# Even stage: five low parts of weight slots made by GpSimd instead of VectorE

## The chip, the cores and the metric

The kernel runs on one core of one Trainium2 chip. The time is that of one execution on the device in microseconds; runs of a kernel are compared by their median. Engines are named as in the profile: PE (TensorE; PEld is its weight load), DVE (VectorE), ACT (ScalarE), POOL (GpSimd), SP (SyncE, which issues the transfers).

## What is computed

Four transformer layers on one sequence of 256 tokens of width 1024, all in float32: two layers of a first block (SwiGLU, a mixer of three branches, SwiGLU), then an "even" layer and an "odd" layer of a second block. The change touches the even layer:

```python
h = rms_norm(x, even_norm_g[i])
proj = h @ even_w_in[i]
q, k, v, z_a, u, z_b = jnp.split(proj, ...)
q = rms_norm(q.reshape(bsz, L, SB_HEADS, SB_HEAD_DIM), sb_q_norm_g[i])
k = rms_norm(k.reshape(bsz, L, SB_HEADS, SB_HEAD_DIM), sb_k_norm_g[i])
o_a = stick_breaking_attention(q, k, v).reshape(bsz, L, SB_WIDTH) * jax.nn.silu(z_a)
o_b = s5_mixer(u, ...) * jax.nn.silu(z_b)      # a diagonal complex state space model, a scan over time
x = x + jnp.concatenate([o_a, o_b], axis=-1) @ even_w_out[i]
```

## The kernel before

**Weights.** All weight matrices are cut into slots of 128 x 2048 float32 (1 MB). A product in full precision is made of three products of a shorter format: each weight w is split into a high part (w copied to fp32r) and a low part (w minus its high part), and `exact3` issues high*high, high*low and low*high (L257 to L259). A slot so goes through four hands: SP loads it into `w_raw` (`load`), ACT copies it to `w_high` (`split_high`, L224), DVE subtracts into `w_low` (`split_low`, L231), and PE multiplies, 48 matmuls for most slots. Three buffers of each kind are used in turn (`RING = 3`): slot n may be loaded when the low part of slot n-3 is made, and its high part may be made when PE is through with slot n-3. Every step waits on a semaphore count; `made(n)` says how many low (or high) parts are made once slot n is.

**Order.** Each engine runs its own list of instructions in the order in which the Python code writes it, and nothing is reordered. The even layer has 29 slots: 0 and 1 give u, 2 and 3 z_b, 4 to 7 z_a, 8 to 11 q, 12 to 15 k, 16 to 19 v, 20 the GLU, 21 to 28 the output. Class `Even` has one method for each engine; each is a loop over n with slot n's own work and, by `after(n)`, the high part (ACT) or low part (DVE) of slot n+3, since slots are three ahead. On DVE an n consists of: the evacuation of slot n's bank (`evac`, L2193 or L2196; for q and k `normalised`, L2203 and L2204), `after(n)`, and at n = 2, 3, 5, 6, 8, 9, 11, 13 one of the eight batches of the state space scan (`scan(0)` to `scan(7)`; at 8, 11 and 13 ahead of `after`). A scan is two products that read PSUM (L2216, L2217; the second releases the PSUM banks, `x_taken`), then ten instructions whose inputs are all in SBUF (L2219, L2220, four scans L2226, L2228 to L2231).

**Who waits for that.** PE, after slot 9, makes the next input of the scans (L2378) into banks that the L2217 of `scan(4)` must have read. In the middle of slots 10 to 17 it transposes a normalised row block (L2358), which needs L2204 and, three times, `skip` (L2236). Before each slot it waits for the low part. ACT makes, in order for each n, the squares and the root for `normalised` (L2078, L2084), the high part of slot n+3, and the silu of z (L2099), which waits for DVE's `evac`.

**GpSimd** works only in the setup and in the two mixers of the first block (bias tables at L1077, windowed sums at L1092). It has nothing to do in the even layer.

Of the kernel before, what the change touches and what calls it, by code (L numbers as in the profile page):

```python
# [19 lines left out]
DEPTH = 2  # L20
# [4 lines left out]
RING = 3  # L25
# [96 lines left out]
class Core:  # L122

    def __init__(self, nc, ctx, weights):
        self.nc = nc
        self.sems = []
        self.ctx = ctx
        self.weights = weights
        sb = lambda name, shape, dt=F32: ctx.enter_context(nc.sbuf_tensor(name, shape, dt))
        self.raw = sb("w_raw", [P, RING, SLOT])  # L130
        self.vec = sb("vectors", [P, V_WIDTH])
        self.tab = sb("table", [P, T_WIDTH])
        self.constants = sb("constants", [P, 2])
# [72 lines left out]
    def made(self, n):  # L206
        return sum(SLOT_PARTS[:n + 1]) + max(n + 1 - len(SLOT_PARTS), 0)

    def load(self, sp, n):
        j = n % RING  # L210
        if n >= RING:
            sp.wait_ge(self.lo_made, self.made(n - RING))
        sp.dma_start(self.raw[:, j, 0:SIZES[n]], self.weights[n][:, 0:SIZES[n]]).then_inc(self.landed[j], 16)
# [12 lines left out]
    def split_low(self, dve, n):  # L226
        if n >= N_SLOTS:
            return
        dve.wait_ge(self.hi_made, self.made(n))
        if n not in self.narrow:  # L230
            dve.tensor_tensor(self.slot(self.wl, n), self.slot(self.raw, n),  # L231
                              self.slot(self.wh, n).bitcast(F32), ALU.subtract).then_inc(self.lo_made, 1)
            return
        gained, gain, f = self.narrow[n]
        if f:
            dve.tensor_tensor(self.slot(self.wl, n)[:, 0:f], self.slot(self.raw, n)[:, 0:f],
                              self.slot(self.wh, n)[:, 0:f].bitcast(F32), ALU.subtract)
        dve.tensor_tensor(gained, self.slot(self.raw, n)[:, f:].rearrange("p (k n) -> p k n", k=DT),
                          gain.unsqueeze(2).to_broadcast([P, DT, QUAD]), ALU.mult).then_inc(self.lo_made, 1)

    def whole(self, n):
# [41 lines left out]
def project(c, pe, bank, n, kt, norm=None, tokens=False, width=FC, x=None, midway=None):  # L283
# [3 lines left out]
    if n >= len(SLOT_PARTS):  # L287
        pe.wait_ge(c.lo_made, c.made(n))
    for k in range(kt):
# [19 lines left out]
def values_half(c, pe, banks, n, half, between=None):  # L309


    wh, wl = c.weights_at(n, DT // 2, 2 * FC)
    pe.wait_ge(c.lo_made, c.made(n))
    for i, bank in enumerate(banks):
# [196 lines left out]
class Ffn:  # L511
# [108 lines left out]
    def tensor(self, pe):  # L620
        c, b, base = self.c, self.b, self.base
# [11 lines left out]
        def down(s):  # L633
            n = base + down_at(s)
            wh, wl = c.weights_at(n, 2, D)
            hh, hl = b.hh[:, s % 2], b.hl[:, s % 2]
            pe.wait_ge(c.lo_made, c.made(n))
            pe.wait_ge(*self.hid_low(s + 1))
# [31 lines left out]
class FfnApart(Ffn):  # L670
# [78 lines left out]
    def tensor(self, pe):  # L749
# [12 lines left out]
        for m in range(FF_STEPS):  # L762
            n = base + 2 * FF_STEPS + m
            wh, wl = c.weights_at(n, SLOT_TILES, FC)
            pe.wait_ge(c.lo_made, c.made(n))
            for p in range(4):
# [279 lines left out]
class Mixer:  # L1046
# [406 lines left out]
    def tensor(self, pe):  # L1453
# [95 lines left out]
        def out_part(n, kks):  # L1549
            u = unit_of(n)  # L1550
            b = bank_free(u) if kks[0] == 0 else unit_bank(u)
            wh, wl = c.weights_at(base + n, DT, FC)
            pe.wait_ge(c.lo_made, c.made(base + n))
            for kk in kks:
# [12 lines left out]
        wh, wl = c.weights_at(n, DT, KV_RANK)  # L1567
        pe.wait_ge(c.lo_made, c.made(n))
        for kk in range(DT):
# [28 lines left out]
        n = base + S_UQ  # L1598
        pe.wait_ge(c.lo_made, c.made(n))
        pe.wait_ge(*t["latent_lo"](2))  # L1600
# [9 lines left out]
        n = base + S_UKV  # L1610
        pe.wait_ge(c.lo_made, c.made(n))
        wh, wl = (c.slot(w, n) for w in (c.wh, c.wl))
# [34 lines left out]
        for n in range(S_BRANCH, S_OUT):  # L1647
# [3 lines left out]
            at = (0, 4, 0)[b]  # L1651
            pe.wait_ge(c.lo_made, c.made(base + n))
            pe.wait_ge(*(t["o_read"](HEADS // 2), t["d_l"](1), t["pool_l"](1))[b])
# [345 lines left out]
class Even:  # L1999
# [326 lines left out]
    def tensor(self, pe):  # L2326
# [8 lines left out]
        def glu(part):  # L2335
            n = base + A_GLU
            wh, wl = c.weights_at(n, UT, S5_W)
            pe.wait_ge(c.lo_made, c.made(n))
            pe.wait_ge(self.y_low, 1)
# [125 lines left out]
        for n in range(A_OUT, EVEN_SLOTS):  # L2465
            b = bank_free(even_unit(n))
            wh, wl = c.weights_at(base + n, EVEN_K, P)
            pe.wait_ge(c.lo_made, c.made(base + n))
            for kk in range(EVEN_K):
# [44 lines left out]
class Odd:  # L2514
# [275 lines left out]
    def tensor(self, pe):  # L2790
# [49 lines left out]
        def heads(n, which):  # L2840
# [3 lines left out]
            wh, wl = c.weights_at(base + n, DT, FC)  # L2844
            pe.wait_ge(c.lo_made, c.made(base + n))
            for h in which:
# [8 lines left out]
        for n in range(G_OUT):  # L2855
# [8 lines left out]
            elif n == G_R:  # L2864
                pe.wait_ge(c.lo_made, c.made(base + n))
                four_columns(pe, c.bank(b, SEQ), c.narrow[base + n][0], c.h).then_inc(c.done, 1)
                self.norm.mean(pe)
            elif n == 0:
                wh, wl = c.weights_at(base, DT, FC)
                pe.wait_ge(c.lo_made, c.made(base))  # L2870
                for kk in range(DT):
# [42 lines left out]
        for n in range(G_OUT, ODD_SLOTS):  # L2914
            if n == G_OUT + 1:
                continue
            if n == ODD_SLOTS - 1:
                b = bank_free(n)
                wh, wl = c.weights_at(base + n, DT, FC)
                pe.wait_ge(c.lo_made, c.made(base + n))  # L2920
                for i in range(2):
# [32 lines left out]
def model_kernel(nc, x, first, pos, table, weights, vectors, second, out):  # L2954
    with ExitStack() as ctx:
# [32 lines left out]
        with nc.Block() as block:  # L2988
# [229 lines left out]
```

## Time and profile before

| what | value |
|---|---|
| median of 3 runs | 1457.62 us (1457.6 to 1457.7) |
| the profiled execution: own time / span | 1457.46 us / 1455.5 us |
| granted TensorE clock | 1.00 throughout |
| PE busy | 1447.2 us, 99% |
| DVE busy | 1057.0 us, 73% |
| ACT busy | 783.2 us, 54% |
| POOL busy | 34.9 us, 2% |
| chain that ended last | PE 93%, DVE 6%, issue 1% |

Busy time is an average over stages; the even layer runs from about 1157 to 1357 us of the span. The profiler's span begins and ends inside the measured time, so an execution's own time is about 2 us more than its span. The span of an instruction includes time in which it is held after it was started. Starts of neighbouring instructions on one engine can overlap the end of the one ahead by some hundredths of a microsecond.

### The profile page before, as it was taken

To read this page: it belongs to the slowest core of one execution; us is meant where nothing else is said; L and a number is where in the kernel's file an instruction comes from. 1 tells how busy PE (TensorE), PEld (TensorE's weight loads), DVE (VectorE), ACT (ScalarE), POOL (GpSimd) and SP (SyncE) were. 2 spreads that over 40 slices of the span, in tenths; PEclk is the share of its full clock that TensorE was granted. 3 is DMA by queue.
4 is the path that set the end of the run, shared out by engine and by line. 5 is a ranking of instruction groups with operands and counts; after the bars stand their busy time and mean duration, and the time that the engine had idled before them with its cause. 6 is when DMAs were issued, how large, how long until landed. Compare 5 with 4: busy or idle time off the path is not lost.

```text
span 1455.5 us, 28504 instructions
## 1 busy us (share of the span) xinstructions
PE 1447.2 (99%) x12414; PEld 1403.4 (96%) x12414; DVE 1057.0 (73%) x1462; ACT 783.2 (54%) x1012; POOL 34.9 (2%) x41
## 2 busy tenths in 40 slices
PE   9999999999999999999999999999999999999999
PEld 9999998999999999999999899999999999989978
DVE  7766676897876655766548689888787799766844
ACT  6444555565554443544446566555645645775753
POOL 0000000210000000000000020000000000000000
PEclk9999999999999999999999999999999999999999
DMA  8655545444555555555554544466555454425541
GB/s 331 225 186 191 191 149 207 145 146 154 194 196 193 201 183 197 200 188 190 201 186 140 194 147 149 170 220 219 203 191 187 149 188 157 145 97 177 198 141 59
DMA packets 38843, 261.36 MB, mean 180 GB/s; under 512 B 4672, under 2 KB 5184, under 8 KB 9152
## 3 DMA queue, kind: packets, MB, share of 16 engines
q1 hardware_dynamic: 38576, 259.54, 52.4%
q8 instruction: 98, 1.61, 0.4%
q14 instruction: 25, 0.20, 0.0%
q10 hardware_dynamic: 144, 0.00, 0.0%
HBM read 258.48 MB, written 1.05 MB: 178 GB/s over the span
## 4 chain that ended last, share of the span: by engine, by line
PE 93%; DVE 6%; issue 1%; ACT 0%; POOL 0%; POOLq 0%
PE ps L257 29%; PE ps L258 28%; PE ps L259 28%; DVE w_low L231 2%; PE ps L1518 1%; DVE scratch L2226 1%; PE ps L1509 0%; PE ps L1491 0%; DVE even_s_rot L2228 0%; PE ps L1533 0%; DVE even_s_rot L2229 0%; DVE even_s_rot L2216 0%; DVE even_s_rot L2217 0%; PE ps L923 0%; PE ps L2812 0%
## 5 line engine op out<-in xcount | busy, mean ns | idle before, releaser
L224 ACT ACTIVATE w_high<-w_raw 128x2048 fp32r<-128x2048 f32 (+1 forms) x243 | 457.3, 1883 | 472.1 <-PE ps L259 469.0
L231 DVE TENSOR_TENSOR w_low<-w_raw,w_high 128x2048 fp32r<-128x2048 f32 (+1 forms) x240 | 545.3, 2273 | 203.2 <-ACT w_high L224 202.8
L257 PE MATMUL ps<-x,w_high 128*128 128x256 f32 x2224 | 622.4, 280 | 0.5 <-DVE w_low L231 0.4
L259 PE MATMUL ps<-x,w_low 128*128 128x256 f32 x2224 | 616.9, 277 | 0.0
L258 PE MATMUL ps<-x,w_high 128*128 128x256 f32 x2224 | 616.7, 277 | 0.0
L257 PEld LDWEIGHTS ps<-x,w_high 128*128 128x128 f32 x2224 | 418.3, 188 | 5.0 <-issue 3.3
L259 PEld LDWEIGHTS ps<-x,w_low 128*128 128x128 f32 x2224 | 418.8, 188 | 0.0
L258 PEld LDWEIGHTS ps<-x,w_high 128*128 128x128 f32 x2224 | 418.5, 188 | 0.3
L257 PE MATMUL ps<-ffn_hid,w_high 128*128 128x256 f32 x528 | 145.7, 276 | 0.0
L258 PE MATMUL ps<-ffn_hid,w_high 128*128 128x256 f32 x528 | 145.7, 276 | 0.0
L259 PE MATMUL ps<-ffn_hid,w_low 128*128 128x256 f32 x528 | 145.7, 276 | 0.0
L257 PEld LDWEIGHTS ps<-ffn_hid,w_high 128*128 128x128 f32 x528 | 99.1, 188 | 0.0
L258 PEld LDWEIGHTS ps<-ffn_hid,w_high 128*128 128x128 f32 x528 | 99.1, 188 | 0.0
L259 PEld LDWEIGHTS ps<-ffn_hid,w_low 128*128 128x128 f32 x528 | 99.1, 188 | 0.0
L257 PE MATMUL ps<-w_high,x 128*128 128x512 f32 (+1 forms) x256 | 87.8, 343 | 0.8 <-DVE w_low L231 0.8
L259 PE MATMUL ps<-w_high,x 128*128 128x512 f32 (+1 forms) x256 | 85.4, 334 | 0.0
L258 PE MATMUL ps<-w_low,x 128*128 128x512 f32 (+1 forms) x256 | 85.4, 334 | 0.0
L257 PE MATMUL ps<-mix_y_high,w_high 128*128 128x256 f32 x224 | 62.6, 279 | 0.8 <-issue 0.8
L259 PE MATMUL ps<-mix_y_high,w_low 128*128 128x256 f32 x224 | 62.3, 278 | 0.0
L258 PE MATMUL ps<-mix_y_low,w_high 128*128 128x256 f32 x224 | 62.3, 278 | 0.0
L257 PEld LDWEIGHTS ps<-w_high,x 128*128 128x128 f32 x256 | 48.1, 188 | 7.9 <-issue 2.4
L259 PEld LDWEIGHTS ps<-w_high,x 128*128 128x128 f32 x256 | 48.0, 188 | 5.2
(478 smaller groups left out, 2086.7 us busy)
## 6 DMA issues: line engine op xcount, KB each, us to landing
w_raw<-in_weights SPq DMA_DIRECT2D x229, 1024.0 KB, 4.9
w_raw<-in_weights SPq DMA_DIRECT2D x10, 768.0 KB, 4.2
setup_first<-in_first SPq DMA_DIRECT2D x8, 256.0 KB, 4.9
w_raw<-in_weights SPq DMA_DIRECT2D x4, 512.0 KB, 5.0
even_second_vectors<-in_second SPq DMA_DIRECT2D x1, 1836.0 KB, 7.4
w_raw<-in_weights SPq DMA_DIRECT2D x2, 640.0 KB, 3.9
resid<-in_x SPq DMA_DIRECT2D x1, 1024.0 KB, 10.7
out<-resid SPq DMA_DIRECT2D x3, 256.0 KB, 3.0
```

The lines of the kernel that those rows point to most:

```text
L224: act.activation(self.slot(self.wh, n)[:, f], self.slot(self.raw, n)[:, f], ACT.Copy).then_inc(self.hi_made, 1)
L231: dve.tensor_tensor(self.slot(self.wl, n), self.slot(self.raw, n), self.slot(self.wh, n).bitcast(F32), ALU.subtract).then_inc(self.lo_made, 1)
L257: pe.matmul(out, ah, bh, start=start, stop=False, skip_group_check=True)
L258: pe.matmul(out, ah, bl, start=False, stop=False, skip_group_check=True)
L259: return pe.matmul(out, al, bh, start=False, stop=stop, skip_group_check=True)
L1518: mm = pe.transpose(c.bank(B_T)[:, i * P:(i + 1) * P], m.pr[:, 0, i * P:(i + 1) * P], ident)
L2226: ins = dve.tensor_tensor_scan(s[:, i, part, :], r, pc[:, i, part, :], 0.0, ALU.mult, ALU.add)
```

## The change

The low parts of the even layer's slots 6, 8, 10, 12 and 14 are made by GpSimd, with the same subtraction of 128 x 2048, in five instructions at the end of its list. They count on a semaphore of their own, `lo_made_pool`. A function `low(n)` gives the semaphore and the count that tell that slot n's low part is made; all waits on it (TensorE, and SyncE ahead of the load of slot n+3) use that. Nothing else is moved.

```diff
@@ constants
+POOL_LOWS = [DEPTH * LAYER_SLOTS + n for n in (6, 8, 10, 12, 14)]
@@ Core
+    def low(self, n):
+
+        if n in POOL_LOWS:
+            return self.lo_pool, POOL_LOWS.index(n) + 1
+        return self.lo_made, self.made(n) - sum(x < n for x in POOL_LOWS)
+
     def load(self, sp, n):
         j = n % RING
         if n >= RING:
-            sp.wait_ge(self.lo_made, self.made(n - RING))
+            sp.wait_ge(*self.low(n - RING))
...
     def split_low(self, dve, n):
-        if n >= N_SLOTS:
+        if n >= N_SLOTS or n in POOL_LOWS:
             return
...
+    def split_low_on_pool(self, pool, n):
+
+        pool.wait_ge(self.hi_made, self.made(n))
+        pool.tensor_tensor(self.slot(self.wl, n), self.slot(self.raw, n),
+                           self.slot(self.wh, n).bitcast(F32), ALU.subtract).then_inc(self.lo_pool, 1)
...
@@ project, values_half and every other place where TensorE waits for a slot
-        pe.wait_ge(c.lo_made, c.made(n))
+        pe.wait_ge(*c.low(n))
@@ block.gpsimd
                 for l in range(DEPTH):
                     stages[3 * l + 1].gpsimd(pool)
+                for n in POOL_LOWS:
+                    c.split_low_on_pool(pool, n)
```

On VectorE, from the end of `scan(3)` to `scan(4)`, before (L2196 is the evacuation of slot 7, L231 the low part of slot 10, L2236 `skip(0)`):

```order
L2230 TENSOR_TENSOR scratch<-even_s_rot 128x2x128
L2231 TENSOR_TENSOR scratch<-even_s_rot 128x2x128
L2196 TENSOR_TENSOR even_za<-ps,rstd 128x512
L231 TENSOR_TENSOR w_low<-w_raw,w_high 128x2048
L2236 SCALAR_TENSOR_TENSOR even_u<-even_u,even_second_vectors,ps 128x256
L2203 RECIPROCAL even_q_sums<-even_q_sums 128x4
L2204 TENSOR_TENSOR even_second_vectors<-ps,even_q_sums 128x512
L2216 TENSOR_TENSOR even_s_rot<-ps,even_cos 128x512
```

and now (line numbers are 8 to 14 higher in the changed file; L2210 is L2196, L2250 is L2236, L2230 is L2216):

```order
L2244 TENSOR_TENSOR scratch<-even_s_rot 128x2x128
L2245 TENSOR_TENSOR scratch<-even_s_rot 128x2x128
L2210 TENSOR_TENSOR even_za<-ps,rstd 128x512
L2250 SCALAR_TENSOR_TENSOR even_u<-even_u,even_second_vectors,ps 128x256
L2217 RECIPROCAL even_q_sums<-even_q_sums 128x4
L2218 TENSOR_TENSOR even_second_vectors<-ps,even_q_sums 128x512
L2230 TENSOR_TENSOR even_s_rot<-ps,even_cos 128x512
```

The low part of slot 10 is gone from between the evacuation and `skip(0)`.

On VectorE, from the end of `scan(4)` to `scan(5)`, before (the first L231 is the low part of slot 11, the second that of slot 12):

```order
L2231 TENSOR_TENSOR scratch<-even_s_rot 128x2x128
L231 TENSOR_TENSOR w_low<-w_raw,w_high 128x2048
L2203 RECIPROCAL even_q_sums<-even_q_sums 128x4
L2204 TENSOR_TENSOR even_second_vectors<-ps,even_q_sums 128x512
L231 TENSOR_TENSOR w_low<-w_raw,w_high 128x2048
L2216 TENSOR_TENSOR even_s_rot<-ps,even_cos 128x512
```

and now:

```order
L2245 TENSOR_TENSOR scratch<-even_s_rot 128x2x128
L239 TENSOR_TENSOR w_low<-w_raw,w_high 128x2048
L2217 RECIPROCAL even_q_sums<-even_q_sums 128x4
L2218 TENSOR_TENSOR even_second_vectors<-ps,even_q_sums 128x512
L2230 TENSOR_TENSOR even_s_rot<-ps,even_cos 128x512
L2231 TENSOR_TENSOR even_s_rot<-ps,even_sin 128x512
```

The low part of slot 11 stays where it was, that of slot 12 is gone.

The end of GpSimd's list before:

```order
L1092 TENSOR_TENSOR mix_arena<-mix_pool_in 128x4x256
L1092 TENSOR_TENSOR mix_arena<-mix_arena 128x3x256
L1092 TENSOR_TENSOR mix_arena<-mix_arena 128x2x256
L1092 TENSOR_TENSOR mix_arena<-mix_arena 128x256
L1077 TENSOR_SCALAR mix_bias<-distance 128x384 x6
```

and now:

```order
L1106 TENSOR_TENSOR mix_arena<-mix_arena 128x3x256
L1106 TENSOR_TENSOR mix_arena<-mix_arena 128x2x256
L1106 TENSOR_TENSOR mix_arena<-mix_arena 128x256
L1091 TENSOR_SCALAR mix_bias<-distance 128x384 x6
L252 TENSOR_TENSOR w_low<-w_raw,w_high 128x2048 x5
```

Five subtractions of 128 x 2048 follow the last bias tables.

## Rows read from the trace of the kernel before

**Rows 1.** Even stage, busy us of PE, PEld, DVE, ACT, POOL; PEclk, DMA share, GB/s.

```profile
1200.00:1250.00 50.00, 48.33 (x521) 46.46 (x520) 46.46 (x81) 27.91 (x75) 0.00 (x0) 1.00 0.41 143
```

**Rows 2.** TensorE timeline: start, us, instruction, [idle before <-releaser].

```profile
1220.74 0.49 PE L2378 MATMUL ps<-even_u,even_b_ahead 32*128 32x128 f32 x4 [0.25 <-DVE even_s_rot L2217]
...
1227.84 0.28 PE L257 MATMUL ps<-w_high,x 128*128 128x256 f32 x1
...
1237.26 0.66 PE L2358 MATMUL ps<-table,even_second_vectors 128*128 128x128 f32 x4 [0.64 <-DVE even_second_vectors L2204]
...
1249.88 0.36 PE L257 MATMUL ps<-w_high,x 128*128 128x256 f32 x1 [0.77 <-DVE w_low L231]
...
1253.29 0.63 PE L2358 MATMUL ps<-table,even_second_vectors 128*128 128x128 f32 x4 [0.34 <-DVE even_u L2236]
```

**Rows 3.** w_low, VectorE, 1155 to 1262 us: ns min/median/max.

```profile
L231 DVE TENSOR_TENSOR w_low<-w_raw,w_high x16: 2271/2282/2293, 1160.3 to 1259.5; 128x2048 fp32r<-128x2048 f32 x16
```

**Rows 4.** DMA issues of the page: KB each, us from issue to landing.

```profile
w_raw<-in_weights SPq DMA_DIRECT2D x229, 1024.0 KB, 4.9
```

**Rows 5.** GpSimd groups by form: busy us, mean ns of one, idle before.

```profile
L1092 POOL TENSOR_TENSOR mix_arena<-mix_pool_in 128x1024 f32<-128x1024 f32 x2 | 3.8, 1894 | 82.0 <-DVE mix_pool_in L1262 82.0
...
L1092 POOL TENSOR_TENSOR mix_arena<-mix_arena 128x512 f32<-128x512 f32 x2 | 2.3, 1168 | 0.2
```

**Rows 6.** Timelines of GpSimd, then of VectorE, in the first mixer.

```profile
261.50 1.89 POOL L1092 TENSOR_TENSOR mix_arena<-mix_pool_in 128x1024 f32<-128x1024 f32 x1 [40.98 <-DVE mix_pool_in L1262]
263.48 3.47 POOL L1092 TENSOR_TENSOR mix_arena<-mix_arena 128x768 f32<-128x768 f32 x1
310.68 1.17 POOL L1077 TENSOR_SCALAR mix_bias<-distance 128x384 f32<-128x384 f32 x1 [5.75 <-DVE mix_max L1284]
...
261.47 0.42 DVE L1284 CUSTOM_DVE_ANT_0 mix_scores<-ps,table 128x256 f32<-128x256 f32 x1
...
261.93 1.49 DVE L1288 TENSOR_SCALAR mix_neg_max<-mix_max 128x2 f32<-128x2 f32 x1
263.34 2.28 DVE L231 TENSOR_TENSOR w_low<-w_raw,w_high 128x2048 fp32r<-128x2048 f32 x1
...
310.71 2.62 DVE L231 TENSOR_TENSOR w_low<-w_raw,w_high 128x2048 fp32r<-128x2048 f32 x1
```

**Rows 7.** ScalarE timeline, even stage: the high parts of slots 6, 8, 10, 12.

```profile
1182.63 1.93 ACT L224 ACTIVATE w_high<-w_raw 128x2048 fp32r<-128x2048 f32 x1 [2.90 <-PE ps L259]
...
1195.94 1.91 ACT L224 ACTIVATE w_high<-w_raw 128x2048 fp32r<-128x2048 f32 x1
...
1207.19 1.91 ACT L224 ACTIVATE w_high<-w_raw 128x2048 fp32r<-128x2048 f32 x1
...
1221.80 1.90 ACT L224 ACTIVATE w_high<-w_raw 128x2048 fp32r<-128x2048 f32 x1
```

**Rows 8.** VectorE timeline, even stage: the scans and their neighbours.

```profile
1184.10 0.69 DVE L2228 TENSOR_TENSOR even_s_rot<-scratch,even_cos 128x512 f32<-128x512 f32 x1
1184.71 0.69 DVE L2229 TENSOR_TENSOR even_s_rot<-scratch,even_sin 128x512 f32<-128x512 f32 x1
...
1186.23 0.69 DVE L2193 TENSOR_TENSOR even_second_vectors<-ps,rstd 128x512 f32<-128x512 f32 x1
...
1190.35 0.43 DVE L2219 TENSOR_TENSOR even_s_rot<-even_s_rot 128x256 f32<-128x256 f32 x1
...
1201.60 0.43 DVE L2219 TENSOR_TENSOR even_s_rot<-even_s_rot 128x256 f32<-128x256 f32 x1
...
1210.05 0.43 DVE L2219 TENSOR_TENSOR even_s_rot<-even_s_rot 128x256 f32<-128x256 f32 x1
...
1220.01 0.68 DVE L2217 TENSOR_TENSOR even_s_rot<-ps,even_sin 128x512 f32<-128x512 f32 x1
...
1225.05 2.29 DVE L231 TENSOR_TENSOR w_low<-w_raw,w_high 128x2048 fp32r<-128x2048 f32 x1
...
1241.79 0.69 DVE L2216 TENSOR_TENSOR even_s_rot<-ps,even_cos 128x512 f32<-128x512 f32 x1 [1.57 <-PE ps L2378]
```

More of the change, by code:

```diff
@@ L147, in __init__ @@
         self.landed = [self.sem(f"landed{j}") for j in range(RING)]
+        self.lo_pool = self.sem("lo_made_pool")
         self.hi_made, self.lo_made, self.done = self.sem("hi_made"), self.sem("lo_made"), self.sem("bank_filled")
@@ L312, in values_half @@
     wh, wl = c.weights_at(n, DT // 2, 2 * FC)
-    pe.wait_ge(c.lo_made, c.made(n))
+    pe.wait_ge(*c.low(n))
     for i, bank in enumerate(banks):
@@ L636, in down @@
             hh, hl = b.hh[:, s % 2], b.hl[:, s % 2]
-            pe.wait_ge(c.lo_made, c.made(n))
+            pe.wait_ge(*c.low(n))
             pe.wait_ge(*self.hid_low(s + 1))
@@ L764, in tensor @@
             wh, wl = c.weights_at(n, SLOT_TILES, FC)
-            pe.wait_ge(c.lo_made, c.made(n))
+            pe.wait_ge(*c.low(n))
             for p in range(4):
@@ L1552, in out_part @@
             wh, wl = c.weights_at(base + n, DT, FC)
-            pe.wait_ge(c.lo_made, c.made(base + n))
+            pe.wait_ge(*c.low(base + n))
             for kk in kks:
@@ L1567, in tensor @@
         wh, wl = c.weights_at(n, DT, KV_RANK)
-        pe.wait_ge(c.lo_made, c.made(n))
+        pe.wait_ge(*c.low(n))
         for kk in range(DT):
@@ L1598, in tensor @@
         n = base + S_UQ
-        pe.wait_ge(c.lo_made, c.made(n))
+        pe.wait_ge(*c.low(n))
         pe.wait_ge(*t["latent_lo"](2))
@@ L1610, in tensor @@
         n = base + S_UKV
-        pe.wait_ge(c.lo_made, c.made(n))
+        pe.wait_ge(*c.low(n))
         wh, wl = (c.slot(w, n) for w in (c.wh, c.wl))
@@ L1651, in tensor @@
             at = (0, 4, 0)[b]
-            pe.wait_ge(c.lo_made, c.made(base + n))
+            pe.wait_ge(*c.low(base + n))
             pe.wait_ge(*(t["o_read"](HEADS // 2), t["d_l"](1), t["pool_l"](1))[b])
@@ L2337, in glu @@
             wh, wl = c.weights_at(n, UT, S5_W)
-            pe.wait_ge(c.lo_made, c.made(n))
+            pe.wait_ge(*c.low(n))
             pe.wait_ge(self.y_low, 1)
@@ L2467, in tensor @@
             wh, wl = c.weights_at(base + n, EVEN_K, P)
-            pe.wait_ge(c.lo_made, c.made(base + n))
+            pe.wait_ge(*c.low(base + n))
             for kk in range(EVEN_K):
@@ L2844, in heads @@
             wh, wl = c.weights_at(base + n, DT, FC)
-            pe.wait_ge(c.lo_made, c.made(base + n))
+            pe.wait_ge(*c.low(base + n))
             for h in which:
@@ L2864, in tensor @@
             elif n == G_R:
-                pe.wait_ge(c.lo_made, c.made(base + n))
+                pe.wait_ge(*c.low(base + n))
                 four_columns(pe, c.bank(b, SEQ), c.narrow[base + n][0], c.h).then_inc(c.done, 1)
@@ L2869, in tensor @@
                 wh, wl = c.weights_at(base, DT, FC)
-                pe.wait_ge(c.lo_made, c.made(base))
+                pe.wait_ge(*c.low(base))
                 for kk in range(DT):
@@ L2919, in tensor @@
                 wh, wl = c.weights_at(base + n, DT, FC)
-                pe.wait_ge(c.lo_made, c.made(base + n))
+                pe.wait_ge(*c.low(base + n))
                 for i in range(2):
```

## The prediction

> **What bounds the kernel now.** I read three things in this order. The busy times of one stretch come first: from 1200 to 1250 us, in the even stage, PE is busy 48.33 us and DVE 46.46 [rows 1]. PE ends the program, so I look for its idle time next: among the moved instructions it waits four times with any weight, 0.25 us for a scan's product, 0.64 us for a normalised row, 0.77 us for the low part of slot 14 and 0.34 us for L2236 [rows 2]. That is 2.0 us. Two things are to be seen here: every releaser is VectorE, and the whole prize is small. VectorE is barely fast enough, and if it is a microsecond later, TensorE stops at these same places for a microsecond more. Third I read what GpSimd and VectorE do to each other in the first mixer, the place where both work [rows 6].
>
> **What moves.** Five subtractions of 128x2048 leave VectorE, where one takes 2.28 us [rows 3]. Its neighbour starts 0.08 us before it ends, as L2229 at 1184.71 does against 1184.10 + 0.69 [rows 8], so each frees 2.2 us of VectorE, 11 us in all. GpSimd, with 0.00 us of work in that stretch [rows 1], gets them. TensorE and SyncE wait as often as before, only on another semaphore: 0 us. The loads of slots 9, 11, 13, 15 and 17 now follow GpSimd's subtraction. By the times below the latest against need is the load of slot 15, issued at about 1231; it takes 4.9 us [rows 4], and slot 15's high part can't be made before TensorE is through with slot 12, after 1237.26 [rows 2]. That cover hides it; without it a late load would hold the high part by as much.
>
> **What one costs on GpSimd.** No row has 2048 elements. 1024 took 1.89 us, 512 took 1.17 [rows 5]. Going on by that step, 0.725 us for 512 elements, gives 1.89 + 1.45 = 3.35 us, the lower end; doubling 1.89 gives 3.79, the upper. VectorE can be held for all of that or a little less. I call the hold H and take **H = 3.4 us**, nearest to the step, with 3.2 and 3.8 as ends.
> The Trainium skill (GPSIMD Engine Reference, "Elementwise — side-by-side cycle accounting") gives 4497 ns for a tensor_tensor of 2048 fp32 elements; this trace's 1024 in 1.89 us speaks for less. By that price the sum below would end near 1466 us.
>
> **Is there room for it?** The high part of slot 12 is made at 1221.80 + 1.90 = 1223.7 us [rows 7]. TensorE starts slot 11 at 1227.84 and is in the middle of slot 12 at 1237.26, after 0.64 us of waiting [rows 2]: 8.8 us for a slot and a half, so slot 12 starts at about 1233.7. That leaves 10 us for an instruction of 3.4 to 3.8. The others have much the same, since slots are made three ahead. So TensorE won't wait for GpSimd; what counts is what GpSimd does to VectorE.
>
> **What they do to each other** [rows 6]. While GpSimd's 1024-element addition ran (261.50 to 263.39), a VectorE instruction on PSUM and one SBUF operand took 0.42 us, but a TENSOR_SCALAR of 2 elements took 1.49 and ended when the addition ended. Then w_low started ahead of GpSimd's 768-element addition: w_low took its usual 2.28 us, the addition 3.47, more than the 1.89 of the larger one. So they take turns, by whole instructions. Where a short GpSimd instruction started just ahead of w_low (310.68 against 310.71), w_low took 2.62: a subtraction with two SBUF inputs is held as well.
> The Trainium skill (SBUF — State Buffer, "Who interferes with whom") has this rule: a VectorE instruction with two SBUF inputs contends with a GpSimd instruction that reads SBUF, the one that comes first keeps the lock to its end, and the other blocks. By that rule, the trace agrees, and it speaks against the change.
>
> **The sum.** In each scan L2216 and L2217 read PSUM, the ten instructions L2219 to L2231 have SBUF inputs alone. I let GpSimd take its turn at the first boundary between two VectorE instructions after its high part is made. Shifts are against before; times of high parts are in rows 7, of VectorE in rows 8.
> - Slot 6: high part ends at 1184.56, within scan 0. VectorE is held 3.4 and saves 2.2: +1.2 us.
> - Slot 8: the high part ended at 1197.85, behind a silu that waits for VectorE's L2196; now 1199.05, so the hold lasts until 1202.45. L2219 of scan 2 stood at 1201.60: +0.9 us.
> - Slot 10: high part, likewise behind a silu, 1209.1 + 0.9 = 1210.0, hold until 1213.4. L2219 of scan 3 stood at 1210.05: +3.4 us. The dropped w_low gives nothing back here, since what follows waits for a chain that starts with the shifted evacuation of slot 7: silu, squares and root on ScalarE, L2204, then L2217 of scan 4, which moves from 1220.01 by 3.4. TensorE waited for that one before [rows 2] and now waits **3.4 us more**.
> - Slot 12: the high part is made at 1227.1, within scan 4, and VectorE is held 3.4 once more. w_low of slot 11 ends at 1227.34 + 3.4 + 3.4 = 1234.1; TensorE wants it at 1227.84 + 3.4 = 1231.2: **2.9 us more**.
> - Slot 14: its turn comes while VectorE waits for TensorE, ahead of 1241.79; it holds nothing. The two w_low dropped at slots 12 and 14 put VectorE ahead, and TensorE gets back 0.64 + 0.77 + 0.34 = **1.75 us**.
> As a formula, (3H - 6.8) + (H - 0.5) - 1.75 = 4H - 9.05 = **+4.55 us**; +3.75 with H = 3.2, +6.15 with 3.8. The profiled execution took 1457.46 us (its span 1455.5, 2.0 lie around it), 0.16 below the median of 1457.62. 1457.46 + 4.55 = **1462.0 us**. A measurement can tell about 0.2% from no change, here 2.9 us.
>
> **Rivals.**
> 1. VectorE keeps its turn while instructions with two SBUF inputs follow each other. For it: each starts before the one ahead ends [rows 8]. Against it: rows 6 show whole instructions taking turns; neither shows GpSimd asking amid such a run. Slot 6 is then made from 1186.23, at L2193, to 1189.6. L2219 of scan 1, due at 1190.35 - 2.2, waits for that: -0.75 us. Slot 8 in the same way holds until 1200.5 against 1201.60: -1.1. Slot 10: high part at 1208.0, hold until 1211.5 against 1210.05: +1.45, all on TensorE as above. Slot 12 waits until scan 4 and w_low of slot 11 are through and holds nobody who matters. 1.45 - 1.75 = -0.3: **1457.2 us**, not slower. What decides is who gets the first boundary inside a scan.
> 2. They don't hold each other in these forms, and VectorE is 2.2 us earlier five times. The four waits go: 1457.46 - 2.0 = **1455.5 us**, still within 0.2%. Rows 6 speak against it. For 2.9 us the stage would have to give more than TensorE idles in it.
> 3. Turns as in the forecast but a longer instruction, since no GpSimd row writes fp32r. A fifth above the upper end is H = 4.4: +8.55, **1466.0 us**.
> 4. The change doesn't do what it says: the orders exclude it.
>
> **Chances.** Forecast 0.50, of which 0.03 come out below 2.9 us; rival 1 0.34, of which 0.03 come out slower with a long H; rival 2 0.07, of which 0.04 go beyond the edge; rival 3 0.09. Slower 0.47 + 0.03 + 0.09 = 0.59, faster 0.04, same 0.37. The range leaves out rival 2 and half of rival 3, about 0.12 in all, and takes in rival 1 with H = 3.2, some 0.7 below its 1457.2: 1456.4 to 1466.0. The forecast's own range is 1461.2 to 1463.6.
>
> **What would show it.** Five GpSimd rows of 128x2048, 3.4 to 3.8 us besides waits. In VectorE's timeline L2228 or L2229 of scan 0 and one such instruction of scan 4 grown to about 4 us, L2219 of scans 2 and 3 grown too. TensorE waiting some 3.6 us at L2378 near 1221 us and 3 us for slot 11's low part, and not at slot 14. If GpSimd's rows stretch to 4 to 8 us instead and no VectorE row inside a scan has grown, rival 1 holds; if neither has, rival 2. If a GpSimd row passes 9 us, TensorE waits for GpSimd itself, and the reasoning is wrong at "is there room".

## The result, and the profile after

The changed kernel takes 1465.87 us (median of 4 runs, 1465.66 to 1466.57) against 1457.66 us for the kernel before (4 runs, 1457.6 to 1458.11): ratio 1.0059, 95% interval 1.0047 to 1.0072, **8.2 us slower**. The forecast was 1462.0, its own range 1461.2 to 1463.6. The direction, the places and the mechanism came as predicted; one term, the length of GpSimd's subtraction, was too small. The profiled execution took 1466.57 us, its span is 1464.4, 8.9 more than before.

The page of the changed kernel, busy times and the chain that ended last (lines of kernel.py are 8 to 14 higher than before: L252 is GpSimd's new subtraction, L239 is w_low, L271 to L273 the products of `exact3`, L2230, L2231, L2233, L2242 to L2245 were L2216, L2217, L2219, L2228 to L2231; L2392 was L2378, L2372 was L2358, and L2407, the products of a finished scan, was L2393):

```profile
PE 1449.9 (99%) x12414; PEld 1405.9 (96%) x12414; DVE 1061.1 (72%) x1457; ACT 782.9 (53%) x1012; POOL 58.6 (4%) x46
...
PE 93%; DVE 5%; issue 1%; ACT 1%; DMA 1%; SPq 0%
```

GpSimd has 23.7 us more, and VectorE, from which 5 x 2.2 = 11 us were taken, is busier than before (1057.0); the chain is TensorE's as before. VectorE's figure can grow although work left it, because an instruction that is held counts as busy while it is held; the rows below show four of these. The stretch of [rows 1] in the changed kernel, same columns:

```profile
1200.00:1250.00 50.00, 42.22 (x397) 40.59 (x396) 45.18 (x64) 22.42 (x54) 15.83 (x4) 0.93 0.39 129
```

VectorE is nearly as busy as in [rows 1] with 64 instructions in place of 81, TensorE got 397 matmuls done in place of 521, and its granted clock fell below 1.00, which nothing in the trace of before had shown. GpSimd's timeline, 1100 to 1300 us (start, us, instruction, idle before and its releaser):

```profile
1184.61 4.78 POOL L252 TENSOR_TENSOR w_low<-w_raw,w_high 128x2048 fp32r<-128x2048 f32 x1 [292.12 <-ACT w_high L232]
1200.26 4.70 POOL L252 TENSOR_TENSOR w_low<-w_raw,w_high 128x2048 fp32r<-128x2048 f32 x1 [10.87 <-ACT w_high L232]
1212.39 4.61 POOL L252 TENSOR_TENSOR w_low<-w_raw,w_high 128x2048 fp32r<-128x2048 f32 x1 [7.43 <-ACT w_high L232]
1230.57 4.96 POOL L252 TENSOR_TENSOR w_low<-w_raw,w_high 128x2048 fp32r<-128x2048 f32 x1 [13.57 <-ACT w_high L232]
1248.44 4.65 POOL L252 TENSOR_TENSOR w_low<-w_raw,w_high 128x2048 fp32r<-128x2048 f32 x1 [12.91 <-ACT w_high L232]
```

They take 4.6 to 5.0 us, not 3.4 to 3.8. VectorE's timeline beside them:

```profile
1184.86 5.08 DVE L2243 TENSOR_TENSOR even_s_rot<-scratch,even_sin 128x512 f32<-128x512 f32 x1
...
1201.73 3.52 DVE L2233 TENSOR_TENSOR even_s_rot<-even_s_rot 128x256 f32<-128x256 f32 x1
...
1212.55 0.68 DVE L2231 TENSOR_TENSOR even_s_rot<-ps,even_sin 128x512 f32<-128x512 f32 x1
1213.26 4.01 DVE L2233 TENSOR_TENSOR even_s_rot<-even_s_rot 128x256 f32<-128x256 f32 x1
...
1231.04 4.77 DVE L2244 TENSOR_TENSOR scratch<-even_s_rot 128x256 f32<-128x256 f32 x1
...
1236.18 2.29 DVE L239 TENSOR_TENSOR w_low<-w_raw,w_high 128x2048 fp32r<-128x2048 f32 x1
```

Four rows have grown: L2243 of scan 0 from 0.69 to 5.08 us, a hold of 4.39; L2233 of scans 2 and 3 from 0.43 to 3.52 and 4.01; L2244 of scan 4 from 0.42 to 4.77, 4.35. Each ends within 0.6 us of a GpSimd row's end. L2231 of scan 3, which reads PSUM, ran through beside GpSimd in its usual 0.68. The four holds make 15.4 us, less the 11 taken away 4.4, and VectorE's busy time grew by 4.1. Slot 14's subtraction held none. And TensorE, each row of the stage with idle time ahead of it, after the start of the scans:

```profile
1213.29 0.49 PE L2392 MATMUL ps<-even_u,even_b_ahead 32*128 32x128 f32 x4 [0.66 <-DVE even_s_rot L2231]
...
1221.19 0.49 PE L2407 MATMUL ps<-even_u,even_b_c 128*128 128x128 f32 x2 [0.90 <-DVE scratch L2245]
...
1227.54 0.80 PE L2392 MATMUL ps<-even_u,even_b_ahead 32*128 32x128 f32 x4 [4.85 <-DVE even_s_rot L2231]
...
1238.62 0.36 PE L271 MATMUL ps<-w_high,x 128*128 128x256 f32 x1 [1.37 <-DVE w_low L239]
```

Against [rows 2]: the product that began at 1220.74 begins at 1227.54, 6.8 later; slot 11's first product, 1227.84, now begins at 1238.62, 10.8 later. The 0.64, 0.77 and 0.34 us at and after slot 12 have no rows any more. 10.8 - 1.75 = 9.0, and the span grew by 8.9.

### The profile page after: what moved, and what is told of

Same layout as the page of the kernel before. It is cut to its first block, busy times and chain, and to the rows that moved or that the text cites. A ratio compares the mean times of both kernels' runs of the same rounds, so it can differ in the third digit from the quotient of the medians.

```text
span 1464.4 us, 28504 instructions
## 1 busy us (share of the span) xinstructions
PE 1449.9 (99%) x12414; PEld 1405.9 (96%) x12414; DVE 1061.1 (72%) x1457; ACT 782.9 (53%) x1012; POOL 58.6 (4%) x46
## 4 chain that ended last, share of the span: by engine, by line
PE 93%; DVE 5%; issue 1%; ACT 1%; DMA 1%; SPq 0%
PE ps L271 29%; PE ps L272 28%; PE ps L273 28%; DVE w_low L239 1%; PE ps L1532 1%; DVE even_s_rot L2233 1%; DVE even_s_rot L2243 1%; DMA w_raw<-in_weights 1%; PE ps L1523 0%; DVE scratch L2240 0%; PE ps L1505 0%; PE ps L1547 0%; PE ps L2826 0%; PE ps L2841 0%; PE ps L2838 0%
## 5 line engine op out<-in xcount | busy, mean ns | idle before, releaser
L239 DVE TENSOR_TENSOR w_low<-w_raw,w_high 128x2048 fp32r<-128x2048 f32 (+1 forms) x235 | 533.8, 2272 | 204.2 <-ACT w_high L232 203.9
L271 PE MATMUL ps<-x,w_high 128*128 128x256 f32 x2224 | 622.4, 280 | 0.9 <-DVE w_low L239 0.4
L273 PE MATMUL ps<-x,w_low 128*128 128x256 f32 x2224 | 616.7, 277 | 0.0
L271 PEld LDWEIGHTS ps<-x,w_high 128*128 128x128 f32 x2224 | 418.4, 188 | 5.4 <-issue 3.3
L273 PEld LDWEIGHTS ps<-x,w_low 128*128 128x128 f32 x2224 | 418.6, 188 | 0.0
L271 PE MATMUL ps<-ffn_hid,w_high 128*128 128x256 f32 x528 | 145.7, 276 | 0.0
L273 PE MATMUL ps<-ffn_hid,w_low 128*128 128x256 f32 x528 | 145.7, 276 | 0.0
L271 PEld LDWEIGHTS ps<-ffn_hid,w_high 128*128 128x128 f32 x528 | 99.1, 188 | 0.0
L273 PEld LDWEIGHTS ps<-ffn_hid,w_low 128*128 128x128 f32 x528 | 99.1, 188 | 0.0
L271 PE MATMUL ps<-w_high,x 128*128 128x512 f32 (+1 forms) x256 | 88.7, 347 | 1.4 <-DVE w_low L239 1.4
L273 PE MATMUL ps<-w_high,x 128*128 128x512 f32 (+1 forms) x256 | 86.1, 337 | 0.0
L271 PE MATMUL ps<-mix_y_high,w_high 128*128 128x256 f32 x224 | 62.6, 279 | 0.8 <-issue 0.8
L273 PE MATMUL ps<-mix_y_high,w_low 128*128 128x256 f32 x224 | 62.2, 278 | 0.0
L271 PEld LDWEIGHTS ps<-w_high,x 128*128 128x128 f32 x256 | 48.9, 191 | 8.7 <-issue 3.6
L273 PEld LDWEIGHTS ps<-w_high,x 128*128 128x128 f32 x256 | 48.8, 191 | 5.2
```

The source lines that it names most:

```text
L271: pe.matmul(out, ah, bh, start=start, stop=False, skip_group_check=True)
L273: return pe.matmul(out, al, bh, start=False, stop=stop, skip_group_check=True)
```

## The experiments

Each is the changed kernel with one edit, except where it says before; "..." stands for lines left out. Times are medians, beside runs of the kernel before on the same chip, whose own medians lay between 1457.32 and 1457.91.

**1. The relief alone.** What do five subtractions fewer on VectorE bring, if nobody makes them?

```diff
-            return self.lo_pool, POOL_LOWS.index(n) + 1
+            return self.hi_made, self.made(n)
...
-                for n in POOL_LOWS:
-                    c.split_low_on_pool(pool, n)
```

`weights_at` gives the high part in place of the missing low one for these five slots, so the results of these five slots lack their low parts.

> The five low parts are left out altogether (TensorE takes the high part a second time in their place and waits for the high part only), so VectorE is relieved as in the change and GpSimd does nothing. Theory (the loss is all due to GpSimd holding VectorE): the four waits of TensorE, 2.0 us, go, and the time is 1455.6 us, 2.0 under before; no VectorE row in the scans is longer than before. Rival (the relief is worth more, or moving work off VectorE costs something by itself, for instance through the loads that start earlier): 1453 or less, or 1457.5 or more.

Measured: 1455.12 us against 1457.91, ratio 0.9982 (0.9973 to 0.9990), 2.8 us faster. The 1200 to 1250 us row:

```profile
1200.00:1250.00 50.00, 50.00 (x538) 48.43 (x538) 39.12 (x72) 29.03 (x75) 0.00 (x0) 1.00 0.41 146
```

TensorE doesn't idle here at all. The prize was small, as the prediction had it (2.0 us of waits); the spans differ by 2.3. The rest, 8.2 + 2.8 = 11 us, is what GpSimd's work costs.

**2. Slot 14 alone, and 3. slot 12 alone.**

```diff
-POOL_LOWS = [DEPTH * LAYER_SLOTS + n for n in (6, 8, 10, 12, 14)]
+POOL_LOWS = [DEPTH * LAYER_SLOTS + n for n in (14,)]
```

and the same with `(12,)`.

> Only slot 14's low part goes to GpSimd. Theory (whole turns, first come first served, a turn of 4.45 us): the high part is made at 1237.4, while w_low of slot 13 (1237.13 to 1239.4) has its turn, so GpSimd runs from 1239.4 to 1243.9, mostly while VectorE waits for TensorE; L2219 of scan 6 is held 0.7 us, w_low of slot 14 is saved, 2.2: the waits at slot 14 and before L2358 (0.77 + 0.34) go, 1456.5 us, 1.1 under before. Rival (GpSimd gets in ahead of w_low of slot 13, or holds more than whole turns): w_low of slot 13 ends 4.4 later, TensorE waits 2 to 3 us for it, 1459 to 1460.

> Only slot 12's low part goes to GpSimd. Theory (turn of 4.45 us at the first boundary within scan 4): w_low of slot 11 ends at 1227.34 + 4.45 = 1231.8 against 1227.84, TensorE waits 4.0 us there and gets 0.64 back before L2358: +3.3, 1460.9 us; if TensorE's clock falls after that wait, up to 2.5 us more. Rival (one turn alone is harmless, the loss of the change needs the three turns before it): within 1 us of before.

Measured for slot 14: 1456.32 us, ratio 0.9988 (0.9979 to 0.9997), 1.6 us **faster** than before. GpSimd, then VectorE:

```profile
1236.36 6.33 POOL L252 TENSOR_TENSOR w_low<-w_raw,w_high 128x2048 fp32r<-128x2048 f32 x1 [344.64 <-ACT w_high L232]
...
1235.89 2.28 DVE L239 TENSOR_TENSOR w_low<-w_raw,w_high 128x2048 fp32r<-128x2048 f32 x1
1241.88 1.10 DVE L2233 TENSOR_TENSOR even_s_rot<-even_s_rot 128x256 f32<-128x256 f32 x1
```

GpSimd waits for the w_low that had started first (to 1238.17), then works 4.5 us, mostly while VectorE waits for TensorE and reads PSUM; only 0.7 us of VectorE is held. TensorE's waits of 0.77 and 0.34 us [rows 2] have no rows any more: 1.1 of the 1.6. Slot 12 alone: 1462.46 us, ratio 1.0035 (1.0022 to 1.0049), 4.5 slower. VectorE's L2244 grows to 4.76 us, slot 11's w_low is late, and TensorE waits; the windows behind it show the clock (columns as in [rows 1]):

```profile
1224.20 4.76 DVE L2244 TENSOR_TENSOR scratch<-even_s_rot 128x256 f32<-128x256 f32 x1
...
1231.77 0.36 PE L271 MATMUL ps<-w_high,x 128*128 128x256 f32 x1 [3.71 <-DVE w_low L239]
...
1232.00:1234.00 2.00, 2.00 (x13) 2.00 (x13) 1.97 (x4) 0.00 (x0) 0.00 (x0) 0.61 0.59 135
1234.00:1236.00 2.00, 2.00 (x12) 2.00 (x12) 1.93 (x7) 0.00 (x0) 0.00 (x0) 0.54 1.04 438
```

3.71 less the 0.64 that is no longer waited for is 3.1 us. In the next 4 us TensorE runs at half clock, 1.2 GHz, most of the time: 2 x 0.39 + 2 x 0.46 = 1.7 us lost. Together 4.8, measured 4.5. So the same instruction is worth -1.6 or +4.5 us, by what VectorE is doing when it comes.

**4. The price without the even stage.** Five slots of the last feed-forward stage (SwiGLU) ahead of the even layer, where TensorE doesn't wait for VectorE.

```diff
+POOL_LOWS = [2 * LAYER_SLOTS - FF_SLOTS + n for n in (3, 6, 9, 12, 15)]
```

> Five low parts of the last feed-forward stage (slots 3, 6, 9, 12, 15 of it) go to GpSimd in place of those of the even stage; VectorE is idle there a third of the time. Theory: each of GpSimd's rows without a wait is 4.6 us, VectorE rows with two SBUF inputs beside them are up to 4.4 longer, and TensorE does not wait: 1457.6 us, within 0.5 of before. It also gives the price of the instruction undisturbed. Rival (the price of 4.6 us seen in the even stage is itself made of contention, the instruction alone is 3.4 to 3.8): GpSimd's shortest rows are 3.4 to 3.8 us. Second rival (turns cost TensorE anywhere): 1460 or more.

Measured: 1458.02 us, ratio 1.0001 (0.9992 to 1.0010): no change. GpSimd, and one VectorE row:

```profile
998.98 4.60 POOL L252 TENSOR_TENSOR w_low<-w_raw,w_high 128x2048 fp32r<-128x2048 f32 x1 [12.44 <-ACT w_high L232]
...
999.45 4.68 DVE L599 TENSOR_TENSOR ffn_hid_low<-ffn_up,ffn_hid_high 128x512 fp32r<-128x512 f32 x1 [1.05 <-ACT ffn_hid_high L545]
```

The subtraction takes 4.60 us where nothing stretches it, so the even stage didn't lengthen it by more than 0.4. A 4 us hold of VectorE happens here too (0.69 is usual at L599), and costs nothing: TensorE isn't waiting for VectorE.

**5. Why 4.6 and not 3.4?** The kernel before, with six additional GpSimd instructions in each mixer, in front of the additions of [rows 5]:

```diff
+        xh, xl = c.xh[:, 0:4, :].bitcast(F32), c.xl[:, 0:4, :].bitcast(F32)
+        c.pool_link(pool.tensor_tensor(pb[:, :, PAD:], xh, xl, ALU.add))
+        c.pool_link(pool.tensor_tensor(pb[:, :, PAD:], xh, xl, ALU.subtract))
+        c.pool_link(pool.tensor_tensor(m.ph[:, :, :], xh, xl, ALU.add))
+        c.pool_link(pool.tensor_tensor(m.ph[:, :, :], xh, xl, ALU.subtract))
+        c.pool_link(pool.tensor_tensor(pb[:, :, PAD:], xh, xh, ALU.add))
+        c.pool_link(pool.tensor_tensor(m.ph[:, 0:2, :], xh[:, 0:2, :], xl[:, 0:2, :], ALU.subtract))
```

> The kernel before, with six more GpSimd instructions in each first-block mixer where it is idle (near 221 us), one after the other, to price the instruction by form: 1024 elements add and subtract into float32, add and subtract into fp32r, add of one tensor to itself, and 512 elements subtract into fp32r. The shortest row of each form counts. Theory A (a subtraction costs 2.2 ns an element whatever its form, and the old additions of 1.89 us for 1024 were cheap for a reason of their own, such as reading one tensor twice): about 2.35 us for all with two tensors, 1.89 for the tensor added to itself. Theory B (writing fp32r is what costs): 1.89 into float32, 2.35 into fp32r. Theory C (subtraction costs more than addition): the split is there.

Measured: 1471.92 us in one execution (before 1457.68); the time isn't the point. GpSimd's timeline in the first mixer, then VectorE's:

```profile
221.06 2.42 POOL L1088 TENSOR_TENSOR mix_arena<-x 128x1024 f32<-128x1024 f32 x1
223.56 4.32 POOL L1089 TENSOR_TENSOR mix_arena<-x 128x1024 f32<-128x1024 f32 x1
227.96 4.33 POOL L1090 TENSOR_TENSOR mix_pool_high<-x 128x1024 fp32r<-128x1024 f32 x1
232.36 2.40 POOL L1091 TENSOR_TENSOR mix_pool_high<-x 128x1024 fp32r<-128x1024 f32 x1
234.84 3.89 POOL L1092 TENSOR_TENSOR mix_arena<-x 128x1024 f32<-128x1024 f32 x1
238.81 1.41 POOL L1093 TENSOR_TENSOR mix_pool_high<-x 128x512 fp32r<-128x512 f32 x1
268.57 1.89 POOL L1099 TENSOR_TENSOR mix_arena<-mix_pool_in 128x1024 f32<-128x1024 f32 x1 [28.36 <-DVE mix_pool_in L1269]
...
223.22 6.80 DVE L231 TENSOR_TENSOR w_low<-w_raw,w_high 128x2048 fp32r<-128x2048 f32 x2 [2.63 <-ACT w_high L224]
229.95 2.35 DVE L1386 TENSOR_TENSOR mix_neg_lam<-mix_lam_s 128x1 f32<-128x1 f32 x1
...
234.70 2.28 DVE L231 TENSOR_TENSOR w_low<-w_raw,w_high 128x2048 fp32r<-128x2048 f32 x1
```

The undisturbed rows decide. An f32 addition of two different tensors takes 2.42 us for 1024 elements, the subtraction to fp32r 2.40: operation and output type are free. The old addition of [rows 5], pool_in with itself shifted by some elements, still takes 1.89. L1092 reads one tensor twice, too: it is held by w_low until 236.98 and ends at 238.73, 1.75 us of its own. So what the prediction's rows lacked was the second tensor. With two, 512 elements cost 1.41 and 1024 cost 2.40 us, 1.0 for 512 more; going on by that step gives 2.40 + 2.0 = 4.4, within 0.2 of the 4.60 measured. The rows also show the turns: GpSimd's L1089 waits for a w_low, the next w_low waits for L1089, L1090 for that w_low, and a VectorE instruction on 128x1 for L1090 (2.35 us).

**6. Shorter turns.** Each subtraction cut into two of 1024 elements.

```diff
+        for f in (slice(0, SLOT // 2), slice(SLOT // 2, SLOT)):
+            ins = pool.tensor_tensor(self.slot(self.wl, n)[:, f], self.slot(self.raw, n)[:, f],
+                                     self.slot(self.wh, n)[:, f].bitcast(F32), ALU.subtract)
+        ins.then_inc(self.lo_pool, 1)
```

> The change with each of the five subtractions cut into two of 1024 elements. Theory (the first in line gets the next turn, whole instructions at a time): VectorE gets one instruction in between and is held 4.4 us in two parts as before, 1465.9 us, within 1 us of the change. Rival (VectorE passes with all that it has ready between the parts, or short turns hold less): 1460 to 1462.

Measured: 1466.26 us, ratio 1.0059 (1.0045 to 1.0073), the same as the change. GpSimd, then VectorE, in scan 0:

```profile
1184.95 5.37 POOL L253 TENSOR_TENSOR w_low<-w_raw,w_high 128x1024 fp32r<-128x1024 f32 x2 [292.58 <-ACT w_high L232]
...
1185.20 2.88 DVE L2245 TENSOR_TENSOR even_s_rot<-scratch,even_sin 128x512 f32<-128x512 f32 x1
1188.11 2.49 DVE L2246 TENSOR_TENSOR scratch<-even_s_rot 128x256 f32<-128x256 f32 x1
```

VectorE gets one instruction in between and is held again: 2.19 + 2.07 = 4.3 us in place of 4.4. What counts is the sum, not the piece.

**7. Slot 10 alone.** Only the tuple changes, to `(10,)`.

> Only slot 10's low part goes to GpSimd. Theory without the clock: GpSimd from 1209.2 to 1213.7, L2219 of scan 3 at 1213.7 instead of 1210.05, all on TensorE at L2378: +3.6, less 0.64 before L2358: 1460.9 us. With the clock (TensorE's granted clock halved for about 5 us after a wait of 3.7 us, as after slot 11's wait in the run with slot 12 alone): some 1.5 more, 1462.4. Rival (slot 10 is harmless by itself since its low part was made early): within 1 us of before.

Measured: 1463.54 us, ratio 1.0041 (1.0027 to 1.0055), 5.9 slower, above both expectations. TensorE and the windows behind it:

```profile
1224.14 0.80 PE L2392 MATMUL ps<-even_u,even_b_ahead 32*128 32x128 f32 x4 [4.06 <-DVE even_s_rot L2231]
...
1231.20 0.60 PE L2372 MATMUL ps<-table,even_second_vectors 128*128 128x128 f32 x4
...
1222.00:1228.00 6.00, 3.86 (x24) 3.64 (x25) 5.83 (x14) 5.06 (x12) 0.00 (x0) 0.67 0.01 1
1228.00:1230.00 2.00, 2.00 (x12) 2.00 (x11) 1.97 (x3) 0.00 (x0) 0.00 (x0) 0.50 0.00 0
1230.00:1232.00 2.00, 2.00 (x16) 2.00 (x16) 1.97 (x4) 0.17 (x1) 0.00 (x0) 0.78 0.33 49
```

4.06 in place of 0.25, less the 0.64 at slot 12 that is gone: 3.2 us from the hold. That leaves 2.7. The row at 1231.20 is the transpose in the middle of slot 10. In the kernel before it stood here:

```profile
1224.66 0.60 PE L2358 MATMUL ps<-table,even_second_vectors 128*128 128x128 f32 x4
```

From the product ahead (1220.74 before, 1224.14 now) TensorE took 3.9 us to it before and takes 7.1 now, with no idle time in it and at the low clock: 3.1 us lost by slow matmuls. Together 6.3, a little above the measured 5.9; this execution came to the stage 0.4 us earlier than the one before.

**8. A GpSimd instruction with one input.** A copy stands in for the subtraction, so the low parts of these slots are left out and their place holds the weights.

```diff
-        pool.tensor_tensor(self.slot(self.wl, n), self.slot(self.raw, n),
-                           self.slot(self.wh, n).bitcast(F32), ALU.subtract).then_inc(self.lo_pool, 1)
+        pool.tensor_copy(self.slot(self.wl, n), self.slot(self.raw, n)).then_inc(self.lo_pool, 1)
```

> The change, but GpSimd copies w_raw to w_low instead of subtracting w_high from it: the same 2048 elements written, one tensor read instead of two (the low part is left out, its place holds the weights). Theory (VectorE is held for as long as GpSimd reads, and reading goes at about 0.9 ns an element, as the 0.34 us for 384 elements in rows 6): H = 1.8 us, and by the formula no loss is left: 1455.5 to 1457 us. Rival (held for the whole of any GpSimd instruction of this size, or the copy takes 4 us too): 1462 to 1466.

Measured: 1456.61 us, ratio 0.9992 (0.9983 to 1.0001), 1.1 us less, hardly told from no change.

```profile
1197.68 1.91 POOL L252 CAST w_low<-w_raw 128x2048 fp32r<-128x2048 f32 x1 [10.84 <-ACT w_high L232]
...
1185.00 2.39 DVE L2242 TENSOR_TENSOR even_s_rot<-scratch,even_sin 128x512 f32<-128x512 f32 x1
```

2048 elements read once take 1.91 us, and hold L2242 for 2.39 - 0.69 = 1.7. With a hold under the 2.2 us that each move frees the loss is gone. The formula of the prediction has 4 x 1.7 - 9.05 = -2.3 for it, twice what was measured, but it doesn't hold for so short a hold: its first part, 3H - 6.8, would be -1.7, and TensorE can get back no more than the 0.25 us that it waited there. With -0.25 in that place the sum is -0.25 + 1.2 - 1.75 = -0.8.

**9. Slots 6 and 8 alone, and 10. all but slot 10.** Tuples `(6, 8)` and `(6, 8, 12, 14)`. Do the prices add up, and do the first two holds reach the end at all?

> The low parts of slots 6 and 8 alone on GpSimd, those of 10, 12 and 14 on VectorE again. The question is whether the first two holds matter to the time at all. The prediction let slot 6 shift VectorE by H minus 2.2, which is 2.2 us at H = 4.4, and that shift stays until something gives it back. Theory A (the shift is carried, since VectorE is the engine TensorE waits for at slots 10 to 14): with the low part of slot 10 on VectorE again nothing gives back the shift before TensorE's product that reads L2217's row, so TensorE stops there some 2 us longer and the time is 1457.7 + 2 to 3 = 1459.7 to 1460.7. Theory B (VectorE waits for TensorE's products between slots 6 and 10, and these waits swallow the shift): between 1456.5 and 1458.5. The whole change gave +8.2 and its slots 10, 12 and 14 alone gave +5.9, +4.5 and -1.6, which add to +8.8: by these sums slots 6 and 8 are worth about -0.6, which speaks for B.

> The change without slot 10: the low parts of slots 6, 8, 12 and 14 on GpSimd. Do the prices of single slots add up? If they do, the whole change's +8.2 less slot 10's +5.9 leaves +2.3, 1460.0 us. By the formula of the prediction, with a hold of 4.4, slot 10's own term falls away and what stays is slot 12's hold less the give-back of 1.75 and whatever shift slots 6 and 8 carry: 4.4 - 0.5 - 1.75 = +2.2 without a carried shift, up to +4.4 with one (1459.9 to 1462.1). The clock: in the run with slot 12 alone TensorE lost its full clock after one wait of 3.7 us; if it does so here too some 1 to 2 us come on top.

Measured: slots 6 and 8 take 1460.89 us, ratio 1.0026 (1.0017 to 1.0035), 3.6 slower; without slot 10, 1463.78, ratio 1.0040 (1.0028 to 1.0053), 6.5 slower. TensorE in the first, with its windows, then in the second:

```profile
1222.87 0.80 PE L2392 MATMUL ps<-even_u,even_b_ahead 32*128 32x128 f32 x4 [2.43 <-DVE even_s_rot L2231]
...
1222.00:1226.00 4.00, 3.13 (x21) 2.91 (x22) 3.90 (x10) 3.79 (x12) 0.00 (x0) 0.57 0.41 168
```

```profile
1212.60 0.49 PE L2392 MATMUL ps<-even_u,even_b_ahead 32*128 32x128 f32 x4 [0.60 <-DVE even_s_rot L2231]
...
1223.26 0.49 PE L2392 MATMUL ps<-even_u,even_b_ahead 32*128 32x128 f32 x4 [2.62 <-DVE even_s_rot L2231]
...
1226.00:1228.00 2.00, 2.00 (x20) 2.00 (x19) 1.97 (x3) 0.30 (x2) 1.70 (x1) 1.00 0.00 0
...
1234.34 0.36 PE L271 MATMUL ps<-w_high,x 128*128 128x256 f32 x1 [3.72 <-DVE w_low L239]
...
1234.00:1236.00 2.00, 1.66 (x14) 1.69 (x15) 1.97 (x5) 0.12 (x1) 0.00 (x0) 1.00 0.49 70
```

Theory B fell. With slots 6 and 8 alone TensorE waits 0.60 us at the scan product ahead (at 1212.20) and 2.43 at this one, in place of 0.25: 2.8 us, and the prediction's shift after slot 8, 2H - 5.95, is 2.85 with H = 4.4. Behind it come slow matmuls: from 1222.87 to the transpose in the middle of slot 10 at 1229.85 TensorE took 7.0 us in place of 3.9.

My argument for B, that single prices add to the whole, was wrong. The single prices 3.6, 5.9, 4.5 and -1.6 add to 12.4, the whole costs 8.2. Two things in the rows keep them from adding. The three slower single runs each pay for a slow stretch behind the wait, 3.1, 3.1 and 1.7 us in their profiled executions (that of experiment 9 lies 1.1 us above its median), where the whole change pays for none in the end, as shown below. And each of the three gets back the 0.64 us at slot 12, which the whole gets back once.

Experiment 10's profiled execution is the clean one: the clock stayed at 1.00 behind all its waits. These, 0.60 + 2.62 + 3.72, less the old 2.0 are +4.9; the terms of the prediction without slot 10's, (2H - 5.95) + (H - 0.5) - 1.75, give 5.0 with H = 4.4. This execution took 1462.04, 4.7 above its neighbours' median, and its span is 4.5 longer than before. Of its other four executions, with mean clocks of 0.997 or 0.998 in place of 1.000, three took 1463.8 to 1463.9 and one 1462.09: a fallen clock goes with up to 1.8 us more, and not in every one.

## Why the prediction was right in its steps and short in one of them

- **What bounds.** Right. TensorE stops at the places named, and every releaser is VectorE. The prize was 2.8 us by experiment 1, against the 2.0 of the waits.
- **What one costs on GpSimd.** This step failed. It extrapolated to 2048 elements from [rows 5] and took 3.4 us, with 3.8 as upper end; the subtraction takes 4.60, and holds VectorE for up to 4.4. As H stands four times in the sum, 1.0 us too little in it makes 4.0 us too little in the forecast. Not the step from 1024 to 2048 was at fault but the rows: both read one tensor twice, where the subtraction reads two (experiment 5). The Trainium skill (GPSIMD Engine Reference, "Elementwise — side-by-side cycle accounting") has 4497 ns for a tensor_tensor of 2048 fp32 elements. The text set it aside with "this trace's 1024 in 1.89 us speaks for less". The runs show 4.60 against the page's 4.50, and the sentence that the sum would end near 1466 by it was the right forecast.
- **Is there room for it.** Right: no wait of TensorE is for GpSimd's subtraction. SyncE does wait for it ahead of its loads, four times, 22.0 us in all, but in the even stage no wait of ScalarE, which reads what is loaded, is for a load.
- **What they do to each other.** Right, and by whole instructions: GpSimd got the next boundary inside a scan, at L2243 of scan 0 and L2244 of scan 4. The rule of the Trainium skill (SBUF — State Buffer, "Who interferes with whom") holds here: the PSUM readers ran beside GpSimd, those with two SBUF inputs stopped.
- **The sum.** Right but for H. The holds inside scans were 4.39 and 4.35. With H = 4.4, (3H - 6.8) is 6.4 and (H - 0.5) is 3.9; measured at the same two rows of TensorE, 6.8 and 10.8 - 6.8 = 4.0. The 1.75 came back in full. 4H - 9.05 = 8.55 gives 1466.0; the median is 1465.87. That these two lie 0.1 us apart is in part luck: the profiled execution grew by 9.1 us and the medians by 8.2. Experiment 10 follows the same terms without slot 10's: 5.0, against 4.9 us of waits.
- **Slot 14.** Right that it holds nobody; alone it is a gain (experiment 2).
- **The rivals.** The size came out as rival 3's (1466.0), whose reason was only half right: the instruction is longer, but not by its fp32r output. Its H = 4.4 was a guess, called a fifth above the upper end of 3.8 (it is a sixth), so that it met the hold to a tenth is luck. The whole range, 1456.4 to 1466.0, takes in the result only by its edge, which was drawn at this rival's value; the forecast's own range misses it by 2.3 us. Rival 1 is refuted by the rows grown within the scans, rival 2 by all of them.
- **Not foreseen.** TensorE waits 0.66 us for scan 3's product, where slot 8's hold arrives, and 0.90 us at L2407, where slot 10's hold delays the end of scan 3. Both are part of the 6.8 and need no term of their own. The fall of the clock is below. In the full change it cost nothing in the end: from 1227.54 to 1238.62 TensorE took 11.1 us in place of 7.1, the forecast H - 0.5; 1.37 of the 4.0 is idle and 2.6 is slowness, and slot 11's low part, ready at 1238.47, would have stopped a fast TensorE as well. So the 3 us of waiting forecast for that place came as 1.37. Experiment 10 shows this case: full clock there, and 3.72 us of waiting.

## What to carry to other kernels

In this kernel an instruction moved from VectorE to GpSimd, both reading SBUF twice, is paid by VectorE itself if VectorE has such instructions waiting: compare the GpSimd duration (here 4.6 us) with the one removed (2.2), not with GpSimd's idle time. Move it where VectorE waits for another engine or reads PSUM; here slot 14 alone made a version that beats both kernels, 1456.32 us, if by only 0.1%. And take an unknown duration from a row with the same operands, not only the same operation and size.

## What the runs showed of the hardware

- **One tensor read twice is cheaper on GpSimd than two tensors.** 1.89 against 2.40 us for 128x1024, 1.17 against 1.41 for 128x512; a copy reads 2048 elements in 1.91. What in the engine or the memory makes the difference was not tried.
- **TensorE's clock can fall at a wait, and then it loses time by slow matmuls as well.** The windows of the changed kernel behind the wait of 4.85 us, columns as in [rows 1]:

```profile
1228.00:1230.00 2.00, 2.00 (x18) 1.77 (x17) 1.93 (x6) 1.97 (x5) 0.00 (x0) 0.50 0.01 4
1230.00:1232.00 2.00, 2.00 (x11) 2.00 (x11) 1.97 (x3) 0.49 (x1) 1.43 (x1) 0.50 0.00 0
1232.00:1234.00 2.00, 2.00 (x16) 2.00 (x15) 2.00 (x1) 0.00 (x0) 2.00 (x1) 0.81 0.00 0
1234.00:1236.00 2.00, 2.00 (x20) 2.00 (x19) 2.00 (x2) 0.69 (x1) 1.53 (x1) 1.00 0.00 0
```

The granted clock is 0.50, the 1.2 GHz level, and 11 matmuls fit in 2 us where 20 do at 1.00. It fell at idle times of 4.85, 4.06, 3.71 and 2.43 us in four kernels (the change, experiments 7, 3 and 9), and stayed at 1.00 after 2.62 and 3.72 in the profiled execution of experiment 10, so the length of the wait alone doesn't decide it; what does stays open. Where nothing hides it, it cost 3.1, 1.7 and 3.1 us (experiments 7, 3 and 9), on top of waits of 4.06, 3.71 and 2.43.
